# Neighbourhood heads of the second block: mixing with the values as stationary operand in f32r, probabilities scaled ahead of it, outcomes produced already turned

## What is computed

```python
h = h + 0.5 * swiglu(rms_norm_2(h, ffn1_norm), ...)
z = rms_norm_2(h, mix_norm) @ w_in
qa, ka, va, qb, kb, vb, ga, gb = split(z)          # 512, 512, 512, 512, 128, 128, 1024, 1024 columns
ya = neighbourhood_attention_2d(qa, ka, va, rpb)   # 8 heads of 64, scores + bias, softmax, times the values
yb = windowed_gqa_sink(rope(qb), rope(kb), vb, sink)  # 8 query heads of 64, 2 key/value heads
merged = sigmoid(ga) * (ya @ w_branch_a) + sigmoid(gb) * (yb @ w_branch_b)
h = h + merged @ w_out
h = h + 0.5 * swiglu(rms_norm_2(h, ffn2_norm), ...)
```

## Time and profile before

| | us |
|---|---|
| median of 3 runs | 960.98 (960.78 to 961.13) |
| the profiled execution | 960.95 |
| its span, first to last instruction | 959.1 |
| PE busy | 951.1 |
| DVE busy | 654.8 |
| ACT busy | 532.1 |
| POOL busy | 59.6 |

### The profile page before, as it was taken

How to read it: one execution, slowest core, us unless ns; L and a number is a source line. 1 busy time by engine, 2 the same in 40 slices (tenths; PEclk the granted TensorE clock), 3 DMA queues, 4 the chain that set the end, 5 groups by cost and what they waited for, 6 DMA issues and landing times.

```text
span 959.1 us, 14069 instructions
## 1 busy us (share of the span) xinstructions
PE 951.1 (99%) x5472; PEld 834.1 (87%) x5472; DVE 654.8 (68%) x837; ACT 532.1 (55%) x688; POOL 59.6 (6%) x94
## 2 busy tenths in 40 slices
PE   9999999999999999999999999999999999999997
PEld 8999988888888888898888888999888898888886
DVE  7778869866665565688666566878656676565664
ACT  7577678436444444474454445678664464444543
POOL 2200000002000000022221000100000020000000
PEclk9999999999999999999999999999999999999999
DMA  9684444553755655547666555644334556655541
GB/s 311 200 258 133 132 132 155 199 179 127 264 197 184 209 175 182 187 157 246 204 216 206 183 181 167 210 142 136 129 133 176 175 171 203 207 187 177 196 153 44
DMA packets 117437, 173.12 MB, mean 180 GB/s; under 512 B 3152, under 2 KB 89440, under 8 KB 117392
## 3 DMA queue, kind: packets, MB, share of 16 engines
q1 hardware_dynamic: 115536, 168.19, 54.0%
q0 software_dynamic: 1424, 3.91, 1.4%
q10 hardware_dynamic: 432, 0.40, 0.1%
HBM read 171.44 MB, written 1.05 MB: 180 GB/s over the span
## 4 chain that ended last, share of the span: by engine, by line
PE 98%; DMA 1%; DVE 0%; issue 0%; POOL 0%; POOLq 0%; SPq 0%; ACT 0%; DVEq 0%
PE pair L674 22%; PE pair L677 11%; PE acc L656 10%; PE acc L658 10%; PE acc L657 10%; PE pair L656 8%; PE pair L658 8%; PE pair L657 8%; PE acc L1176 1%; PE acc L1021 1%; PE pair L873 1%; PE acc L1162 1%; PE acc L790 1%; PE acc L856 1%; DMA xt<-in_x 1%; PE pair L720 0%
## 5 line engine op out<-in xcount | busy, mean ns | idle before, releaser
L674 PE MATMUL pair<-actp,wh 128*128 128x512 f32 x912 | 292.8, 396 | 0.0
L1706 DVE TENSOR_TENSOR wl<-raw,wh 128x2048 fp32r<-128x2048 f32 x89 | 204.9, 2303 | 62.7 <-ACT wh L1281 62.7
L1281 ACT ACTIVATE wh<-raw 128x2048 fp32r<-128x2048 f32 x88 | 168.4, 1914 | 83.7 <-PE acc L658 83.7
L677 PEld LDWEIGHTS pair<-actp,wl 128*128 128x128 f32 x912 | 171.3, 188 | 39.9
L677 PE MATMUL pair<-actp,wl 128*128 128x256 f32 x912 | 179.2, 278 | 0.0
L1701 DVE TENSOR_TENSOR wl<-raw,wh 128x2048 fp32r<-128x2048 f32 x68 | 155.4, 2288 | 30.2 <-ACT wh L1275 29.9
L1275 ACT ACTIVATE wh<-raw 128x2048 fp32r<-128x2048 f32 x69 | 132.1, 1916 | 76.9 <-PE pair L658 54.2
L674 PEld LDWEIGHTS pair<-actp,wh 128*128 128x128 f32 x912 | 141.6, 189 | 1.4
L1494 ACT ACTIVATE arena<-pair 128x512 f32<-128x512 f32 x57 | 34.0, 597 | 170.8 <-PE pair L674 170.8
L656 PE MATMUL acc<-wh,midh 128*128 128x512 f32 x312 | 121.7, 390 | 0.0
L658 PE MATMUL acc<-wh,midl 128*128 128x512 f32 x312 | 121.4, 389 | 0.0
(11 more groups left out here) (334 smaller groups left out, 1373.7 us busy)
## 6 DMA issues: line engine op xcount, KB each, us to landing
raw<-in_w_in SPq DMA_DIRECT2D x37, 1024.0 KB, 5.2
raw<-in_mlp_w SPq DMA_DIRECT2D x32, 1024.0 KB, 5.4
raw<-in_ffn_w_gate SPq DMA_DIRECT2D x22, 1024.0 KB, 5.3
raw<-in_ffn_w_up SPq DMA_DIRECT2D x22, 1024.0 KB, 5.3
raw<-in_ffn_w_down SPq DMA_DIRECT2D x22, 1024.0 KB, 4.9
raw<-in_w_out SPq DMA_DIRECT2D x8, 1024.0 KB, 4.8
raw<-in_w_up_rnn SPq DMA_DIRECT2D x4, 1024.0 KB, 5.1
raw<-in_cmp_k_w SPq DMA_DIRECT2D x2, 1024.0 KB, 6.2
```

The costliest lines, as they stand in the source:

```text
L674: return nc.tensor.matmul(bank[:, :].rearrange("p (u t) -> p u t", u=2), h[:, k, cs], actp[:, :, k, :], **kw)
L677: return nc.tensor.matmul(bank[:, 0:T], l[:, k, cs], acth[:, k, :], **kw)
L1281: nc.scalar.activation(wh[:, n % R, :], raw[:, n % R, :], ACT.Copy).then_inc(hi_ready, 1)
L1706: nc.vector.tensor_tensor(wl[:, n % R, :], raw[:, n % R, :], wh[:, n % R, :].bitcast(F32), ALU.subtract).then_inc(lo_ready, 1)
```

## The change

Only the neighbourhood heads (k < 8) are computed in another way:

- The probabilities are scaled before they are turned: DVE takes the reciprocal when the exponential is done (`coef2`), ACT multiplies `prob2` by it (`scale2`, two instructions), and only then PE may turn them.
- The turned probabilities are split into an f32r high part `pth` (ACT, `copy2`) and a low part `ptl` (DVE, `low_probs`).
- The values are kept as high and low side by side, 128 columns for each head and key tile (`vals`: ACT writes the high, DVE the low), and are the stationary operand of the mix: four f32r matmuls of 256 columns. Rows 0 to 63 of bank 4 then hold the high values' share, rows 64 to 127 the low values' share.
- ACT copies the lower rows (`low_rows`), DVE adds both to `yaT`, features on partitions (`norm2`). The two `turn_out` calls for `atok2` go.
- For room, queries and keys a have one buffer for both halves, the high and low query rows of heads 4 to 7 reuse those of heads 0 to 3, and the copies and low parts of queries move to later places. `exp2` and `scale2` stand ahead of `hi(n+2)` on ACT in iterations +3 to +10, and `lo` runs one panel later on DVE from +3 to +10 (`low_at`), with two in iteration +11.

The diff, cut to what the text speaks of:

```diff
@@ PE
             def turn2_(k):
-                pe.wait_ge(exped, NH + k + 1)
-                pe.wait_ge(probT_ready, NH + k)
+                if k < NH:
+                    pe.wait_ge(scaled, k + 1)
+                else:
+                    pe.wait_ge(exped, NH + k + 1)
+                if 0 < k <= NH:
+                    pe.wait_ge(ptl_ready, k)
...
             def mix2(k):
+                vt = head2(k)[3]
+                if k < NH:
+
+                    pe.wait_ge(ptl_ready, k + 1)
+                    pe.wait_ge(normed, NH + k)
+                    if k % 4 == 0:
+                        pe.wait_ge(val_ready, k // 2 + 2)
+                    for kt in range(TT):
+                        for pt in (pth, ptl):
+                            m = nc.tensor.matmul(ps[4][:, 0:T], vt[kt], pt[:, kt, :], start=kt == 0 and pt is pth,
+                                                 stop=kt == 1 and pt is ptl)
+                    m.then_inc(mixed, 1)
+                    return
...
-                if n == GA2:
-                    pe.wait_ge(normed, NH + 4)
-                    pe.wait_ge(vb_ready, 1)
-                    turn_out(OUT_A, atok2, 0)
-                if n == GA2 + 3:
-                    pe.wait_ge(normed, 2 * NH)
-                    pe.wait_ge(midl_ready, 2)
-                    turn_out(OUT_A, atok2, 2)
@@ ACT
+            def low_rows(k):
+
+                act.wait_ge(mixed, NH + k + 1)
+                act.wait_ge(normed, NH + k)
+                nc.scalar.activation(ylow[0:DH, :], ps[4][DH:2 * DH, 0:T], ACT.Copy).then_inc(ylow_ready, 1)
+
+            def scale2(k):
+
+                act.wait_ge(coef_ready, k + 1)
+                o = k % 3
+                for tt in range(TT):
+                    m = nc.scalar.activation(prob2[:, tt, :], prob2[:, tt, :], ACT.Copy, scale=coef[:, o, tt:tt + 1])
+                m.then_inc(scaled, 1)
...
+                early = VA2 <= n - 1 <= GA2
+                if early:
+                    heads2_turned(n - 1, 1)
                 if n - 1 in KA2:
...
+                if early:
+                    heads2_scored(n - 1, 1)
...
+                if n - 1 == KA2[1]:
+                    act.wait_ge(scored, NH + 4)
+                    queries_hi(qaT, 0)
                 hi(n + 2)
...
+                if n in (GA2 + 1, GA2 + 3):
+                    u = int(n > GA2 + 1)
                     act.wait_ge(qb_ready, u + 1)
-                    act.wait_ge(scored, NH + 4 * u + 4)
-                    queries_hi(qbT, u)
+                    act.wait_ge(scored, NH + 8)
+                    if u:
+                        act.wait_ge(mixed, NH + 8)
+                    queries_hi(both(qbT, u), u)
@@ DVE
+            def coef2(k):
+
+                dve.wait_ge(exped, NH + k + 1)
+                o = k % 3
+                nc.vector.reciprocal(coef[:, o, 0:TT], sums[:, o, 0:TT]).then_inc(coef_ready, 1)
+
+            def low_probs(k):
+
+                dve.wait_ge(probT_ready, NH + k + 1)
+                nc.vector.tensor_tensor(ptl.rearrange("p k t -> p (k t)"), ps[3][:, :],
+                                        pth.rearrange("p k t -> p (k t)").bitcast(F32), ALU.subtract).then_inc(ptl_ready, 1)
...
+            low_at = {VA2 + 1: []}
+            low_at.update({n: [n + 1] for n in range(VA2 + 2, GA2 + 2)})
+            low_at[GA2 + 2] = [GA2 + 3, GA2 + 4]
...
                 heads2(n - 1, 1)
+                if n - 1 == KA2[1]:
+                    keys2_lo(1)
...
+                heads2_late(n - 1, 1)
...
+                if n - 1 == KA2[1]:
+                    queries_lo(qaT, 0, 4)
                 if n < F2 - 1:
-                    lo(n + 2)
+                    for m in low_at.get(n, [n + 2]):
+                        lo(m)
```

More of the change, by code:

```diff
@@ L359, in build @@
         va_evac = sem("va_evac")
+        val_ready = sem("val_ready")
+        coef_ready = sem("coef_ready")
+        scaled = sem("scaled")
+        ptl_ready = sem("ptl_ready")
+        ylow_ready = sem("ylow_ready")
         qb_evac = sem("qb_evac")
@@ L605, in parity, with both @@
             return v[:, 4 * u + odd:4 * u + 4:2, :]
+        def both(v, u):
+            return v[:, 2 * u:2 * u + 2, :]
         def own(odd):
@@ L1589, in heads2, with heads2_scored @@
                     return
+                if 0 <= k - 2 < NH:
+                    low_rows(k - 2)
                 if 0 <= k - 1 < 2 * NH:
                     copy2(k - 1)
+            def heads2_scored(n, part):
+                k = turn2.get((n, part))
+                if k is None:
+                    return
                 if k < 2 * NH:
                     exp2(k)
+                if k < NH:
+                    act.wait_ge(exped, NH + k + 1)
+                    scale2(k)
             def out_hi(dst, i, bank, count):
@@ L1629, in _ @@
                         for half in range(2):
-                            nc.scalar.activation(parity(keys2(u)[0][own(half)], 0, odd), kaT[own(odd), 2 * u:2 * u + 2, :],
+                            nc.scalar.activation(parity(keys2(u)[0][own(half)], 0, odd), kaT[own(odd)],
                                                  ACT.Copy).then_inc(kst_hi, 1)
+                if n in (VA2 + 2, KBVB + 1):
+                    u = int(n > VA2 + 2)
+                    done(VA2 + 1)
+                    act.wait_ge(rstd_ready, TT * 4)
+                    if u:
+                        act.wait_ge(scored, NH + 4)
+                    for tt in range(TT):
+                        nc.scalar.activation(vals(u, tt)[:, :, 0, :], va_bank(u, tt), ACT.Copy, scale=rstd[:, tt:tt + 1]).then_inc(va_evac, 1)
+                if n - 1 == KBVB:
+                    act.wait_ge(kv_evac, 1)
+                    act.wait_ge(nab_ready, 8)
+                    swap(swk, kbT[:, :])
+                if n - 1 in (QB, QB + 1):
+                    u = n - 1 - QB
+                    act.wait_ge(qb_evac, u + 1)
+                    swap(swq[:, u, :], qbT[:, 2 * u:2 * u + 2, :].rearrange("p a t -> p (a t)"))
+                if early:
+                    heads2_scored(n - 1, 1)
                 if n == QB + 1:
@@ L2184, in heads2, with heads2_late @@
                     return
+                if 0 <= k - 2 < NH:
+                    norm2(k - 2)
                 if k < 2 * NH:
                     mask2(k)
-                if 0 <= k - 2:
+                if 0 <= k - 1 < NH:
+                    low_probs(k - 1)
+                if k - 2 >= NH:
                     norm2(k - 2)
+            def heads2_late(n, part):
+                k = turn2.get((n, part))
+                if k is not None and k < NH:
+                    coef2(k)
             def rope(x, swapped, r1, r2, width, done_count):
@@ L2208, in out_lo, with keys2_lo @@
                                         ALU.subtract).then_inc(midl_ready, 1)
+            def keys2_lo(u):
+                kh, kl = keys2(u)
+                for odd in range(2):
+                    for half in range(2):
+                        dve.wait_ge(kst_hi, 4 * u + 2 * odd + (1 + odd if half == 0 else 2))
+                        m = nc.vector.tensor_tensor(parity(kl[own(half)], 0, odd), kaT[own(odd)],
+                                                    parity(kh[own(odd)], 0, odd).bitcast(F32), ALU.subtract)
+                m.then_inc(kst_ready, 1)
+            low_at = {VA2 + 1: []}
+            low_at.update({n: [n + 1] for n in range(VA2 + 2, GA2 + 2)})
+            low_at[GA2 + 2] = [GA2 + 3, GA2 + 4]
             for n in range(QKV2, F2):
```

134 lines of the change are left out of this document (69 added, 65 removed).

## The result

| | before | after |
|---|---|---|
| median, us | 961.06 (960.78 to 961.5, 4 runs) | 973.62 (972.32 to 975.89, 4 runs) |
| ratio after to before, 95% interval | | 1.0134 (1.0121 to 1.0146) |
| the profiled execution / its span | 960.95 / 959.1 | 975.89 / 974.1 |
| mean granted clock of its runs | | 0.991, 0.993, 0.993, 0.995 |

The account below looks back on a forecast made before the run. PE, busy 951.1 of 959.1 us, was taken to bound the kernel. Waits of 14.7 us less 3.8 saved give +10.9, from 960.95 to 971.8 us; own range 968.5 to 974.5, with rivals partly included 964.5 to 975.5.

Parts of the forecast that it names:

- the forecast's own case: Whole kernel: waits for DVE and ACT outweigh PE's saving at clock 1.00, giving 971.8 us; 62%.
- rival (d): Clock falls too: each 3.5 us stretch of work costs about 1.75 more, partly swallowed; two give 973.5 to 977; 10%.
- What PE saves: Eight new mixes save 2.9 us and the dropped turns of outcomes 0.9: PE's own work falls by 3.8 us.
- The new operations: Per head on ACT and DVE: lower rows 0.4, scaled pair 0.85, low probabilities 0.65, norm 0.43; values' parts about 0.8, twice.
- First late place: Panel +7: DVE's query lows and `lo(+7)` end at 645.65, so PE starts it 3.3 us late.
- Second: Slot 7 and panel +10: PE waits for low and scaled probabilities, 3.9 us late, after 0.3 at panel +9.
- the ring: ACT and DVE waiting on each other in turn, from panel +7 to slot 7: a chain of 24.3 us, until 670.0.
- Third: Slot 8: DVE's query lows end at 681.0 while PE is there at 677.6, 3.5 us late.
- Fourth: Slots 9 to 11: 0.3 late at slot 9, 1.7 at slot 10's turn, 1.65 at slot 11's turn.
- (a): The cover holds: ACT and DVE hand over fast enough that nothing is late, 957.2 us; 8%.
- (b): Only panel +7 is late and the later lists have slack: 960.5 us; 6%.
- Rival (c): Late until slot 7, then recovered, as the b queries come in time: 964.7 us, up to 968; 14%.

Follow-up runs that it names:

- with filler: Changed kernel with unneeded f32r matmuls put on PE where it waits, and the wait for `vb_ready` at slot 7's start: 972.14 us, ratio 1.0118.
- The experiment with the mix alone: Kernel before with the neighbourhood heads' mix replaced, on PE alone, by four f32r matmuls on other data: 958.40 us, ratio 0.9974.
- the DMA kernel: Changed kernel, order untouched, with ACT's three swaps for rope as four DMAs each from POOL's queue: 969.48 us, ratio 1.0098.
- the kernel with the end reordered: Changed kernel with `lo(+13)` behind slot 9's mask and the second b queries' copies and low parts moved later: 968.57 us, ratio 1.0087.
- with iteration +6 reordered: Changed kernel with queries ahead of keys on ACT and DVE, reciprocal between key lows, `lo(+7)` at the end of iteration +5: 971.12 us, ratio 1.0107.
- the best kernel: Changed kernel with iteration +6, the end and further places reordered, and the rope swaps as DMAs: 960.14 us, ratio 0.9992.

## Why the prediction was right, and where it was short

Direction and mechanism were right: 971.8 was forecast and 973.62 came, 1.8 us above the forecast's own case and just inside what rival (d) had, 973.5 to 977. The table takes the lengths of slots and panels, start to start in PE's timeline, less the length without a wait (1.39 for a slot with a new mix, 1.76 for one with an old one, 2.74 for half a token panel, 5.76 and 5.59 for panels +7 and +10).

| lost, us | forecast | with filler, clock 1.00 | after |
|---|---|---|---|
| ahead of panel +7 | 3.3 | 3.3 | 3.3 |
| panel +7 itself | 0 | 0.1 | 2.8 |
| panel +9, slot 7 | 0.3 + 3.9 | 3.7 | 2.9 |
| panel +10 itself | 0 | 0 | 1.3 |
| slot 8 | 3.5 | 3.5 | 2.2 |
| slot 9 and the half panel behind | 0.3 | 0.8 | 0.7 |
| slot 10 | 1.7 | 1.6 | 1.6 |
| ahead of and in slot 11 | 1.65 | 1.7 | 2.4 |
| the half panel behind slot 11 | 0 | 0 | 0.9 |
| sum | 14.7 | 14.7 | 18.1 |

Less the 3.75 that PE saves, 18.1 gives 14.4; with the 0.44 us that the profiled execution of after is late already at its first score (614.41 against 613.94), that is 14.8 of its 975.89 - 960.95 = 14.9. These 0.44 us have nothing to do with the change: they are there in full in DVE's timeline at 44 us of the span, and the profiled executions of the other kernels stand between 0.25 us ahead of the kernel before and 0.25 behind it at the first score. With filler it is 14.7 - 3.75 = 10.95, and the spans differ by 970.2 - 959.1 = 11.1.

- **What PE saves** (3.8): right. In after the mixes give eight times 0.37, the turns of outcomes 0.35, 0.35 and 0.1: 3.75. The experiment with the mix alone has 2.5 of its 3.0.
- **The new operations.** The scaled pair took 0.91 (0.85 said), the lower rows 0.38 (0.4), the low probabilities 0.69 (0.65), the norm 0.42 (0.43), a pair of the values' low parts 0.86 (0.8). None of them is a surprise; their order is what costs.
- **First late place**: 3.3 said; 646.09 - 641.41 - 1.40 = 3.28. Query lows were walked to start at 642.0 and started at 642.32; `lo(+7)` was to end at 645.65 and ended at 646.03, in a profile that ran 0.46 us behind the walk from slot 3 on.
- **Second**: the ring was walked to 3.9 late at slot 7, and 0.3 ahead of it. With the clock at 1.00 it is 3.7, and the 0.3 doesn't show: 0.5 too much was booked here. That the ring runs through the swaps is shown by the DMA kernel.
- **Third**: 3.5 said, 3.5 measured at clock 1.00, 2.2 in after, where PE comes later because the clock fell in panel +10: 1.3 + 2.2 is the same 3.5.
- **Fourth**: 0.3, 1.7 and 1.65 said; 0.8, 1.6 and 1.7 came at clock 1.00. Of the 0.8, the two `lo` of iteration +11 make the 0.3 in the half panel behind slot 9 (3.03 us; 2.75 in the kernel with the end reordered, which parts them). The other 0.46 lies in slot 9 itself, stays there, and ends with ACT's exponentials: 0.5 too little was booked in this place.
- **The total at clock 1.00**: 971.8 forecast, 972.14 measured with filler. Panel +13 was to start at 702.9 and starts at 703.03 there. That the sums agree to 0.1 us is in part luck, since the 0.5 too much at slot 7 and the 0.5 too little at slot 9 cancel; each term by itself is within 0.5.

**The step that was short is the clock.** The forecast kept 1.00 and gave rival (d) 10%, yet (d) is what happened, in part: three stretches at half clock in the profiled execution, behind the waits of 1.32 and 1.56 us, behind that of 2.50, and behind those of 0.87 and 0.38. They cost 2.7 + 1.3 + 0.9 us in panels and some 0.9 us inside slots 7 and 11 (the turn at 699.88 takes 1.03 us where the one at 693.66 takes 0.66), 5.8 in all; the waits are 12.3 us in place of 14.7 in return, since PE comes later to data that DVE and ACT pace. Place by place against the kernel with filler, the stretch of panel +7 reaches the end with 1.9 us and that of slot 11 with 1.6, while that of panel +10 is swallowed whole by slot 8. In the median the clock is worth 973.62 - 972.14 = 1.5 us. Of the mechanism of (d) both halves are thus borne out: the extra time and its being swallowed in part. The price of (d) is the weak part. The length of 3.5 us was an assumption that no row of before shows, and 1.75 more holds for 3.5 us of time at half clock; 3.5 us of work, as it says, would take 3.5 more. Measured were 2.7 us more for the first stretch and 1.3 for the second.

Rivals (a) and (b) fall by the table. Rival (c), the b queries in time, falls by the 3.5 at slot 8.

**What stays open.** Why the clock falls behind a given wait in one execution and not in another: the same waits of 1.3 and 1.6 us were followed by a clock of 1.00 in the profile of the kernel with the end reordered, and by a fall in that of the kernel with DMA swaps (panel +7 took 5.86 and 7.33 us). Behind 2.55 us in slot 7 panel +10 took 5.58 us with iteration +6 reordered and 7.19 with the end reordered; behind 3.3 us in slot 8 the half panel took 4.34 and, with DMA swaps, 2.76. Nor was after ever run with the old lead of `lo` given back and all else left: that the late `lo` is harmless in the kernel before doesn't show what it costs beside the new head work, where panel +7 does wait for it. And the 3.0 us of small waits left in the best kernel are read from its profile, not taken away one by one.

## What to carry to other kernels

When one engine bounds the kernel and two others feed it in turn, count the handovers in their lists, not their busy shares: here lists that were 83 to 87% busy came late once each head needed one more round trip from ACT to DVE and back. Put work that waits for nobody ahead of the instruction that waits: with orders changed so and the swaps off ACT, the loss of 12.6 us went to none. And expect that a late place mended early in the ring for the most part comes back behind it (1.0 of 2.7 us was kept), while one at its end is a net gain (3.6 of 3.6). Price each new idle time of TensorE a second time for the clock, and then ask whether a wait behind it takes that back: here it did behind panel +10 and didn't behind panel +7.

## What the runs showed of the hardware

- **Half clock behind short waits.** After idle times of 1.32 and 1.56 us, parted by a score of 0.7 us, TensorE's granted clock was 0.50 of full, 1.2 in place of 2.4 GHz, in the window from 647 to 649, and a panel of 48 matmuls took 8.54 in place of 5.76 us. After one idle time of 2.50 us a panel took 6.92 in place of 5.59. After 1.96 us at slot 8 it stayed at 1.00; in other kernels' profiles it fell behind 3.30 us and stayed at 1.00 behind 3.27. The Trainium skill, "TensorE: Matmul & The Clock Gate", section "HAM oscillation — how this bites in real kernels", says that idle gaps between bursts of matmuls can put the engine back to half its clock. The trace of after agrees in kind, with the numbers above; the waits in that section's example are of some 3 to 5 us, those named here were of 1.3 to 3.3 us, and the clock fell behind such waits in some executions only.
- **Filler is worth its matmuls.** With filler in the waits the clock was 1.00 in every window of 2 us of the stage, the median fell by 1.5 us and the spread of the runs from 3.6 to 0.36 us (four runs each).
- **Copies between partitions.** 32x512 in f32: 0.64 us on ACT, 1.8 us on POOL as `tensor_scalar`, and 2.1 us from issue to landing as a DMA of 64 KB, which the page counts as busy time of no engine.
- **An f32 mix against an f32r one.** Eight records of 64 columns in plain f32 took 0.84 us, four f32r matmuls of 256 columns 0.48.
